# Head projections reordered: keys and values first, the query's convolution and key-query products inside the inverse, one tap on ScalarE

## The reference, cut to what matters

```python
px = hx @ w_in                                   # latent tokens; context: keys and values only
kvq_x = silu(latent_conv(px[..., COL_K:COL_Z], conv_w))      # 5 taps along the tokens, per channel
k = l2norm(heads(kvq[..., :DN_WIDTH])); v = ...; q = l2norm(...) * DN_HEAD_DIM ** -0.5
# per chunk: decay from cumulated gates, then
lmat = where(strict, (kb @ kc.T) * decay, 0)
sol  = triangular_solve(lmat + I, [v*b, kb*exp(gc)])
attn = where(incl, (qc @ kc.T) * decay, 0)
# scan over chunks
v_new = u_i - w_i @ s
o_i   = qd_i @ s + a_i @ v_new
s     = s * exp(gl_i) + kd_i.T @ v_new
```

## Time and profile before

| what | us |
| --- | --- |
| median of three runs | 2537.08 |
| lowest and highest | 2532.02, 2538.87 |
| the profiled execution, its own time | 2534.12 |
| span of that execution | 2532.0 |
| TensorE busy | 2293.3 (91%) |
| VectorE busy | 1742.3 (69%) |
| ScalarE busy | 812.4 (32%) |
| GpSimd busy | 1205.9 (48%) |

### The profile page before, as it was taken

How to read it: one execution, slowest core, us unless ns; L and a number is a source line. 1 busy time by engine, 2 the same in 40 slices (tenths; PEclk the granted TensorE clock), 3 DMA queues, 4 the chain that set the end, 5 groups by cost and what they waited for, 6 DMA issues and landing times.

```text
span 2532.0 us, 36784 instructions
## 1 busy us (share of the span) xinstructions
PE 2293.3 (91%) x12290; PEld 1934.5 (76%) x12290; DVE 1742.3 (69%) x3343; ACT 812.4 (32%) x1271; POOL 1205.9 (48%) x682
## 2 busy tenths in 40 slices
PE   6798998998899999949999698999898999999995
PEld 2578777777877687739999698998897777777774
DVE  3666666666664211055577998787855999999999
ACT  3423323323332232223334243333333333333331
POOL 0313212312312144314457686555567787777873
PEclk9899999999999999979999899999999999999997
DMA  5311211111111132223347686787879988998883
GB/s 219 102 49 55 76 54 61 60 62 63 63 56 53 62 124 97 83 100 119 118 144 246 194 263 241 281 314 307 312 301 382 349 318 324 334 337 328 324 311 138
DMA packets 149391, 470.11 MB, mean 186 GB/s; under 512 B 14544, under 2 KB 47536, under 8 KB 148144
## 3 DMA queue, kind: packets, MB, share of 16 engines
q1 hardware_dynamic: 110176, 302.32, 34.3%
q0 software_dynamic: 36864, 134.23, 14.1%
q10 hardware_dynamic: 2256, 32.51, 3.2%
HBM read 414.43 MB, written 54.58 MB: 185 GB/s over the span
## 4 chain that ended last, share of the span: by engine, by line
PE 51%; DVE 22%; issue 14%; DMA 6%; POOL 3%; ACT 2%; DVEq 1%; ACTq 0%; SPq 0%; POOLq 0%
PE bank L534 10%; PE bank L536 9%; PE bank L535 9%; DVE pair L1787 6%; DMA rows<-peer_u,e_row 4%; PE bank L1845 3%; PE bank L1980 3%; PE bank L1973 3%; POOL w_lo L1072 2%; DVE c_lo L1774 2%; PE bank L2283 2%; DVE cv L1297 2%; DVE rows L1661 1%; DMA raw<-w 1%; PE bank L1937 1%
## 5 line engine op out<-in xcount | busy, mean ns | idle before, releaser
L1072 POOL TENSOR_TENSOR w_lo<-raw,w_hi 128x1024 fp32r<-128x1024 f32 x208 | 509.8, 2453 | 809.2 <-ACT w_hi L712 427.5
L534 PE MATMUL bank<-lat_hi,w_hi 128*128 128x384 f32 (+1 forms) x1536 | 565.2, 368 | 28.5 <-ACT gu L984 9.5
L536 PE MATMUL bank<-lat_hi,w_lo 128*128 128x384 f32 (+1 forms) x1536 | 548.9, 357 | 0.0
L535 PE MATMUL bank<-lat_lo,w_hi 128*128 128x384 f32 (+1 forms) x1536 | 548.6, 357 | 0.0
L1072 POOL TENSOR_TENSOR w_lo<-raw_more,w_hi 128x1024 fp32r<-128x1024 f32 x136 | 328.0, 2412 | 196.9 <-ACT w_hi L912 116.8
L1768 DVE TENSOR_TENSOR cf<-gl,gq 128x384 f32<-128x384 f32 x128 | 327.1, 2556 | 11.2 <-DMA gq<-g_dram 5.7
L534 PEld LDWEIGHTS bank<-lat_hi,w_hi 128*128 128x128 f32 x1536 | 294.4, 192 | 48.9 <-issue 30.5
L536 PEld LDWEIGHTS bank<-lat_hi,w_lo 128*128 128x128 f32 x1536 | 293.0, 191 | 21.6
L535 PEld LDWEIGHTS bank<-lat_lo,w_hi 128*128 128x128 f32 x1536 | 294.2, 192 | 17.0
L2302 PE MATMUL bank<-w_hi,c_hi 128*128 128x512 f32 x768 | 251.4, 408 | 2.9 <-DVE c_lo L1774 2.8
L2302 PE MATMUL bank<-w_hi,c_lo 128*128 128x512 f32 x768 | 239.4, 393 | 0.0
(11 more groups left out here) (345 smaller groups left out, 3719.4 us busy)
## 6 DMA issues: line engine op xcount, KB each, us to landing
raw<-w SPq DMA_DIRECT2D x208, 512.0 KB
raw_more<-w SPq DMA_DIRECT2D x136, 512.0 KB
gu_dram<-gu SPq DMA_DIRECT2D x128, 192.0 KB
g_dram<-gs ACTq DMA_DIRECT2D x6, 4096.0 KB, 16.5
gl<-gu_dram SPq DMA_DIRECT2D x16, 1536.0 KB
gq<-g_dram SPq DMA_DIRECT2D x16, 1536.0 KB
ada<-w_ada SPq DMA_DIRECT2D x32, 512.0 KB, 3.3
dY<-gc_dram SPq DMA_DIRECT2D x8, 768.0 KB, 4.0
```

Source lines behind the costliest of these rows:

```text
L534: nc.tensor.matmul(out, hi, rh, start=start, stop=False)
L535: nc.tensor.matmul(out, hi, rl, start=False, stop=False)
L536: return nc.tensor.matmul(out, lo, rh, start=False, stop=stop)
L1072: nc.gpsimd.tensor_sub(w_lo[:, slot, :], raw_at(slot % 2 if src is None else src), w_hi[:, slot, :].bitcast(F32)).then_inc(split_done, 1)
```

## The change

The order of a head's projections becomes K_LAT, K_CTX, V_LAT, V_CTX, Q_LAT, Z_LAT, with the weights laid out accordingly and other PSUM banks. The centre tap of each convolution is made by ScalarE (`middle_tap`), which reads its weight from a small tile that VectorE fills once a head (`middle_weights`). V_CTX is convolved in step 4. The query's four other taps, its silu and square, the key-query products, and all four attention products move into the inverse. All tokens are transposed at the end of the scan (`values_lat`, `keys_by_token`). At level 0 the masked tile W is transposed instead of Lt, and VectorE adds the result to X straight from PSUM, without a mask on that side. The wait for the last XT moves from the end of the inverse to behind the first projection blocks of the scan. GpSimd scales all chunks' keys in two instructions, and splits the fourth weight tile inside the inverse.

The core of the diff:

```diff
-        K_LAT, K_CTX, Q_LAT, V_LAT, V_CTX, Z_LAT = range(6)
-        P_BANK = (1, 0, 7, 1, 0, 7)
+        K_LAT, K_CTX, V_LAT, V_CTX, Q_LAT, Z_LAT = range(6)
+        P_BANK = (1, 0, 7, 0, 1, 7)
...
+            def middle_tap(n, o):
+                lat = o in (K_LAT, V_LAT, Q_LAT)
+                size = SEQ if lat else CTX
+                act.wait_ge(proj, n * 6 + (o + 1))
+                act.wait_ge(mid_w, n + 1)
+                act.wait_ge(silu, n * 5 + max(o - 1, 0))
+                nc.scalar.activation(cv[:, o % 2, 0:size], bank[P_BANK[o]][:, 0:size], ACT.Copy,
+                                     scale=cwm[:, P_KIND[o]:P_KIND[o] + 1]).then_inc(center, 1)
...
+            def first_masked(n, g):
+                dve.wait_ge(lt, (n + 1) * (NG + NCH))
+                nc.vector.tensor_tensor(W[:, 3 * g:3 * g + 3, :], Lt[:, 3 * g:3 * g + 3, :],
+                                        rep(cst[:, C_LVL:C_LVL + P], 3), ALU.mult).then_inc(mask_t, 1)
...
@@ VectorE, level 0 @@
             def first_plain(n, g):
-                mask = rep(cst[:, C_LVL:C_LVL + P], 3)
                 dve.wait_ge(mx_mm, n * 14 + (g + 1))
-                nc.vector.tensor_tensor(T[:, 3 * g:3 * g + 3, :], bank[5 + g][:, 0:3 * P].rearrange(b4, b=P), mask,
-                                        ALU.mult).then_inc(t_done, 1)
                 dve.wait_ge(id_done, n * 5 + 1)
-                dve.wait_ge(t_done, n * 14 + (g + 1))
-                nc.vector.tensor_tensor(x_v, x_v, as_pairs(flat3(T[:, 3 * g:3 * g + 3, :]), 0), ALU.add).then_inc(x_done, 1)
+                nc.vector.tensor_tensor(x_v, x_v, as_pairs(bank[3 + g][:, 0:3 * P], 0), ALU.add).then_inc(x_done, 1)
...
@@ VectorE @@
             def inverse(h, fin):
+                tap = conv_of(h, Q_LAT)
...
+                    if lv == 1:
+                        tap(0)
                     if lv == 2:
-                        output_norms(h, fin, bank[4][:, 3 * P:3 * P + LAT])
+                        tap(2)
+                        tap(3)
+                        if fin:
+                            output_norms(h - 1, bank[4][:, 3 * P:3 * P + LAT])
...
+                    if lv == 1:
+                        tap(1)
+                    if lv == 3:
+                        attention(h, 0)
+                        attention(h, 1)
...
@@ TensorE, inverse @@
                     if lv == 1:
                         pe.wait_ge(z_done, h + 1)
-                        pe.wait_ge(conv, h * 5 + 5)
+                        pe.wait_ge(kev, h * 2 + 2)
+                        pe.wait_ge(vev, h * NCH + NCH)
...
-                pe.wait_ge(xt_done, h * 14 + 14)
...
@@ TensorE, fill of the scan @@
                     if (s, slot) == (5, 2):
-                        coupling_transposed(n)
+                        first_plain(n)
+                    if (s, slot) == (5, 1):
+                        values_lat(n)
                     if (s, slot) == (5, 2):
-                        keys_lat(n)
+                        keys_by_token(n)
```

More of the change, by code:

```diff
@@ L873, in next_head @@
                 identity_xt(CT + 1, 2 * NCH - 1)
+                middle_tap(n, Q_LAT)
                 act.wait_ge(solve, h * 12 + 12)
@@ L876, in next_head @@
                 identity_xt(2 * NCH - 1, 2 * NCH)
-                silu_of(n, V_CTX)
+                values(n, range(CT, NCH), bank[5])
                 next_hi(n, 2)
                 silu_z(n)
-                next_hi(n, 3)
                 keys_lat(n)
+                keys_ctx(n)
+                values(n, range(CT), bank[6][:, CTX:])
                 square_o(h)
+            middle_tap(0, K_LAT)
+            middle_tap(0, K_CTX)
             silu_of(0, K_LAT)
+            middle_tap(0, V_LAT)
             silu_of(0, K_CTX)
@@ L887, in _ @@
             next_hi(0, 0)
-            silu_of(0, Q_LAT)
-            next_hi(0, 1)
-            square_q(0)
+            middle_tap(0, V_CTX)
             identity_x(0)
@@ L896, in _ @@
             silu_of(0, V_CTX)
+            next_hi(0, 1)
+            middle_tap(0, Q_LAT)
+            values(0, range(CT, NCH), bank[5])
             next_hi(0, 2)
             silu_z(0)
-            next_hi(0, 3)
             keys_lat(0)
+            keys_ctx(0)
+            values(0, range(CT), bank[6][:, CTX:])
             inverse(0, False)
@@ L1092, in next_weights @@
                 lengths(n)
-                for j in range(1, 4):
+                for j in range(1, 3):
                     lo(j, n * 4 + (5 + j))
@@ L1275, in conv_of @@
             def conv_of(h, o):
-                kind, lat = (0, 0, 2, 1, 1)[o], o in (K_LAT, Q_LAT, V_LAT)
+                kind, lat = P_KIND[o], o in (K_LAT, V_LAT, Q_LAT)
                 n_row, row = (SEQ // GRID_W, GRID_W) if lat else (1, CTX)
@@ L1455, in scan @@
                 for s in range(NCH):
-                    tap = conv_of(n, s - 1) if more and s else None
+                    conv_on = more and 1 <= s <= 4
+                    tap = conv_of(n, s - 1) if conv_on else None
                     if s:
@@ L2108, in _ @@
             project(0, K_CTX, range(KB))
-            project(0, Q_LAT, range(0, 6))
+            project(0, V_LAT, range(0, 6))
             pe.wait_ge(gate_done, 2)
@@ L2123, in _ @@
             key_products(0, range(CT, NCH))
-            project(0, V_CTX, range(KB))
+            project(0, Q_LAT, range(KB))
             pe.wait_ge(key_norm, 1)
```

278 lines of the change are left out of this document (141 added, 137 removed).

## The result

After the change the kernel takes 2453.33 us, the median of four runs (2451.49 to 2456.83), beside 2534.55 (2523.23 to 2538.87) for four runs of the kernel before on the same chip: ratio 0.9688, 95% interval 0.9653 to 0.9723. Five more runs gave 2456.85 (2450.53 to 2458.58), ratio 0.9707, interval 0.9686 to 0.9729. The sign and the mechanism were right, the gain was forecast as 59 us and is 77 by the two profiled spans (2532.0 and 2455.0).

What follows compares the result with a forecast made beforehand. TensorE, with its waits and slow clock, was taken to bound the kernel: 10.0 - 0.95 - 1.7, say 7.4 us a period, 52 over seven, plus 7 in the opening, 59 off, giving 2476 us (range 2460 to 2504).

Steps and rivals of the forecast that it cites:

- case C: Scan steps 1 to 4: late ScalarE centre taps hold Vn, the state and TensorE's next product; 2559 us, chance 0.06.
- The opening: Head 0 before its inverse: couplings end 2.5 us earlier, masks and collisions save 4.5; together 7 us, bounds 2.5 and 9.8.
- the costs added: Per head period: new TensorE waits, 0.95 us from ScalarE's tail and 1.7 from VectorE's added work in the inverse.
- the time removed: Per head period: 7.5 us of TensorE waits and 2.5 of slow clock go, 10.0 in all.
- ScalarE's tail: ScalarE's work after Z's projection, before the first level: TensorE newly waits 0.7 to 1.2 us, taken as 0.95.
- VectorE's new work in the inverse: Query taps and attention products in the inverse: TensorE waits 0.55 and 0.3 us for X, 0.85 for a mask; 1.7.
- 7.5 of waits: TensorE's waits per head period expected to go: 2.4 + 2.1 + 1.3 + 1.0 + 0.7 us; one of 0.2 stays.
- 2.5 of slow clock: First level, each period: TensorE groups at the 1.2 GHz level after idling, about 2.5 us over full speed, expected to go.
- Case E: ScalarE's tail and VectorE's taps cost nothing: 10 us a period and 9.8 in the opening; 2454 us, chance 0.05.
- Rival A: Before the first level: GpSimd's w_lo collides with VectorE's XT add, 2 to 3 us a period; 2490 to 2496, chance 0.18.
- B: VectorE bounds the inverse: all 3.9 us exposed, ScalarE's tail 1.2; gain 4.9 a period, total 2494 us, chance 0.14.
- D: TensorE finds another late result at each place; half of the 10.0 us a period comes back; 2514 us, chance 0.08.

Runs made afterwards that it cites:

- the one with eight copies: The changed kernel with eight scratch VectorE copies (128x512 from PSUM, never read), all ahead of the first level's first X; 2509.63 us in one run.

## Why the prediction was wrong, step by step

**What held.** Every wait that was to go is gone: 2.4 and 2.1 for X, 1.3 for Rd, 1.0 behind the attention product, 0.7 for XT, and with them the stretch at 0.50. The order of VectorE's work before the first X is as forecast (4.8 us against "some 4"). The centre taps on ScalarE cost nothing, at 0.69 for 512 columns. Steps 1 to 4 of the scan got no wait, so the slower case C did not come. The opening gave 8.0 where 7 stood. Behind 840 us nothing changed beyond what one execution differs from another. Which part of the change took the waits for Rd and behind the attention product was not tried by itself; the lists show only that they are gone.

**The steps that failed.** The mechanism was right; two terms of the sum were mis-sized, the costs added (2.65) and the time removed (10.0). First the costs. The forecast charged 0.95 for ScalarE's tail and 1.7 for VectorE's new work in the inverse, 2.65. Measured: 0.68 for W; 0.41 for the taps of Q instead of 0.85 (0.48 with the taps left out); 0.63 for the attention products instead of 0.85. That is 1.72 by the rows, 0.9 too much in the sum. (W's new wait also has a piece that its row does not show: the group ahead of it, at 364.06, shows its full 0.88, and the one behind it is followed after 0.77, where 0.67 is the rule. That is 0.3 more and would make the costs 2.0.) Half of the 0.9 is the taps of Q: the lateness of the first X add was carried in full to the second. Behind taps 2 and 3 VectorE's adds follow each other like this:

```profile
372.88 0.55 DVE L1455 TENSOR_TENSOR X<-X,bank 128x384 f32<-128x384 f32 x1
373.35 0.55 DVE L1458 TENSOR_TENSOR XT<-XT,bank 128x384 f32<-128x384 f32 x1
373.81 0.55 DVE L1455 TENSOR_TENSOR X<-X,bank 128x384 f32<-128x384 f32 x1
374.27 0.55 DVE L1458 TENSOR_TENSOR XT<-XT,bank 128x384 f32<-128x384 f32 x1
```

They start every 0.46, not every 0.55, and TensorE delivers a group every 0.67: a late VectorE wins back 0.2 with each add, 0.4 by the second X add (373.81), which starts four tenths less late than the first (372.88). The other two costs are not of this kind, since the forecast had priced them by the distance of starts. For the attention products it took each op to end just as the next may start; the kernel before already waits 0.24 at level 3 behind one product of 0.39, the changed kernel 0.63 behind two, so 0.15 of each such stretch is covered. And ScalarE's tail, which answers to the earlier trace rows, came out 0.2 shorter than forecast:

```profile
362.76 0.60 ACT L807 ACTIVATE dn<-bank 128x512 f32 x1 [1.11 <-PE bank L540]
363.25 0.58 ACT L813 COPY Kn<-bank 128x512 f32<-128x512 f32 x1
...
364.97 1.07 ACT L852 COPY TW<-XT 128x384 f32<-128x384 f32 x2
```

TensorE starts behind W 2.87 us after the tail begins (362.76 to 365.63), where the forecast had 3.1; the wait is 0.68, the lower end of its 0.7 to 1.2.

**The other term: what is removed.** It was 10.0 and is some 11.2 in the steady period: 9.5 gained plus the 1.7 that came. The forecast made it of 7.5 of waits and 2.5 of slow clock. The waits are 7.7 by their rows, with the 0.2 that I kept and that went too. The slow clock is 2.1 by the starts of its groups, and not 2.5: it was added up from the lengths of rows that overlap, in one head, while the waits came from another. What is left, some 1.4, the forecast put at nothing: the time next to a wait that the wait's row does not show. The run with XT's wait moved shows 0.25 of it for one wait. For the other four nobody measured it alone; at 0.25 each five waits would make 1.2, an estimate from that one.

**In the sum**: by the mean of all seven gaps 9.3 instead of 7.35, that is 2.0 too little a period (0.9 of costs and 1.1 of what is removed), 2.0 x 7 = 14 us, and 2 to 3 in the opening and the first inverse: 75 by the end of the heads for 59. The remaining 2 are unedited stretches, 3 lost and 5 won. The range's lower end (2460) had been set by the bounds of the forecast alone (2463). Case E (2454) had a chance of 0.05, and that the time came out at its figure is luck: E has no new waits, and there are 1.7 of them.

**The other cases.** Rival A was close. In the steady heads the XT adds run from 359.54 and 360.99, the second ending (361.91) 0.2 behind the start of w_lo at 361.73 and escaping it. In head 0 the order is the other way; GpSimd and then VectorE there:

```profile
121.42 2.37 POOL L1097 TENSOR_TENSOR w_lo<-raw,w_hi 128x1024 fp32r<-128x1024 f32 x1 [1.71 <-ACT w_hi L717]
```

```profile
121.96 2.56 DVE L1378 TENSOR_TENSOR XT<-XT,TW 128x384 f32<-128x384 f32 x1
```

TensorE waits 2.13 us for what stands behind it, which is one cause why the first gap is larger and scatters. The changed kernel, and then the one with eight copies (whose head 0 has none of them), have the same stop there and another sequel:

```profile
125.30 0.99 PE L1986 MATMUL bank<-X,Lt 128*128 128x128 f32 x6 [2.13 <-DVE X L1385]
126.12 0.83 PE L2013 MATMUL bank<-TW 128*128 128x128 f32 x6
```

```profile
122.80 1.65 PE L1994 MATMUL bank<-X,Lt 128*128 128x128 f32 x6 [2.11 <-DVE X L1391]
124.25 1.48 PE L2021 MATMUL bank<-TW 128*128 128x128 f32 x6
```

B fell with the run without query taps, C and D by the lists of waits.

## What to carry to other kernels

Price a chain of short operations on the engine that feeds the bottleneck by the distance of their starts, not by the length of their rows, and compare that distance with the bottleneck's own: a feeder that is faster wins a delay back within a few operations. Price a wait by the distance of the starts on both sides of it, since its row left out 0.25 us at the one place where it was measured. Judge edits of a loop body by its steady period, without the first pass, when an unedited tail of the program varies by more than the edit is worth. And read a clock's loss from all passes of the loop, since the same waits gave between 0 and 2.9 us of it.

## What the runs showed of the hardware

- TensorE's granted clock after a stop is not a fixed price. Stops of 0.3 and 2.1 us were followed by no slow group in two heads and by up to 2.9 us of loss in five; a single stop of 2.1 us in head 0 did nothing in one kernel and brought 1.65 for 0.83 in another; a single stop of 3.3 us or more brought it in all seven heads, and so did 1.9 + 1.7. Stops of 0.7 and 0.6 in a period never did.
- The wait for the last XT cost more than its row, 0.97 us by the starts where the row has 0.72: the end of the twelve matmuls ahead of it (L1980, 1.50 long) is overlapped by their successor only where that does not wait (1.26 from start to start).
- Short gaps hide as busy time: the groups at 373.48 and 374.41 are 0.94 long where their like take 0.83, and the list of waits shows nothing, yet the 0.41 between the starts is what leaving the taps out gives back (0.48).
- A strided add into X from PSUM takes 0.88 to 0.93 at the first level and 0.56 at the next (366.60, the same size from the same memory): the first level's pairs cost more, from SBUF as well (XT at 359.54, 0.86), which the forecast had as its upper end (0.86).
